# One stage for the last step of the third mixer branch and the output projection

## What is computed

```python
def rwkv7_group(p, ...):
    ...
    _, o = lax.scan(chunk_step, state0, xs)
    o = o.reshape(S, B, H, N).transpose(1, 0, 2, 3)
    mean = jnp.mean(o, axis=-1, keepdims=True)
    var = jnp.mean(jnp.square(o - mean), axis=-1, keepdims=True)
    o = ((o - mean) * lax.rsqrt(var + GN_EPS)).reshape(B, S, RWKV_WIDTH) * ln_g + ln_b
    bonus = jnp.sum(rh * kh * r_k, axis=-1, keepdims=True) * vh
    return (o + bonus.reshape(B, S, RWKV_WIDTH)) * g

def second_block(x, ...):
    ...
    y = jnp.concatenate([ya, yb.astype(x.dtype), yc.astype(x.dtype)], axis=-1)
    x = x + (y @ w_out[l]).astype(x.dtype)
    x = x + hier_moe(rms_norm_2(x, norm2_g[l]), ...)
```

## Time and profile before

| what | us |
|---|---|
| median of 3 runs | 2276.52 |
| lowest and highest of them | 2267.41, 2284.37 |
| the profiled execution | 2268.78 |
| its span, first to last instruction | 2266.9 |

### The profile page before, as it was taken

The page is one execution under the profiler, slowest core; times in us unless marked ns, Lnnn a source line. Parts: engine busy times, 40 slices in busy tenths (PEclk is TensorE's granted clock), DMA queues, the critical chain, the costliest instruction groups (busy, mean ns, idle before and its releaser), DMA issues. The chain is left out here.

```text
span 2266.9 us, 33009 instructions
## 1 busy us (share of the span) xinstructions
PE 2121.3 (94%) x12489; PEld 1633.1 (72%) x12489; DVE 1271.5 (56%) x1796; ACT 985.9 (43%) x1297; POOL 178.6 (8%) x178
## 2 busy tenths in 40 slices
PE   7988898999999999998999999998999789998998
PEld 5764334788888878888887888786577359777776
DVE  3357746443233244434666666888367755525888
ACT  2127636342123221121666665774253643414774
POOL 0010000000000000001211000012112210002111
PEclk9999989999999999999999999999999899998999
DMA  8008001243234135013887877995320000127996
GB/s 252 18 19 290 1 19 38 65 131 99 81 100 126 38 101 173 1 38 107 271 282 273 288 268 277 374 391 217 102 75 29 12 1 1 76 86 224 380 375 254
DMA packets 221008, 337.14 MB, mean 149 GB/s; under 512 B 50445, under 2 KB 135470, under 8 KB 220895
## 3 DMA queue, kind: packets, MB, share of 16 engines
q1 hardware_dynamic: 213758, 315.27, 41.0%
q0 software_dynamic: 7136, 20.34, 2.5%
HBM read 307.56 MB, written 26.95 MB: 148 GB/s over the span
## 5 line engine op out<-in xcount | busy, mean ns | idle before, releaser
L1550 DVE TENSOR_TENSOR moe_pass_wL<-moe_pass_w,moe_pass_wH 128x2048 fp32r<-128x2048 f32 (+1 forms) x144 | 303.3, 2112 | 113.6 <-ACT moe_pass_wH L1474 113.3
L1474 ACT ACTIVATE moe_pass_wH<-moe_pass_w 128x2048 fp32r<-128x2048 f32 (+1 forms) x144 | 254.7, 1772 | 129.8 <-PE PS L568 92.5
L1550 DVE TENSOR_TENSOR hm_pass_wL<-hm_pass_w,hm_pass_wH 128x2048 fp32r<-128x2048 f32 x60 | 135.8, 2286 | 37.0 <-ACT hm_pass_wH L1474 37.0
L566 PE MATMUL PS<-moe_pass_wL,moe_pass_xgH 128*128 128x512 f32 (+1 forms) x384 | 147.3, 384 | 7.4 <-DVE moe_pass_wL L1550 5.0
L568 PE MATMUL PS<-moe_pass_wH,moe_pass_xgH 128*128 128x512 f32 (+1 forms) x384 | 142.7, 372 | 0.0
L567 PE MATMUL PS<-moe_pass_wH,moe_pass_xgL 128*128 128x512 f32 (+1 forms) x384 | 142.6, 371 | 0.0
L568 PE MATMUL PS<-ffn_xH,ffn_upH 128*128 128x512 f32 x352 | 139.7, 397 | 0.0
L566 PE MATMUL PS<-xnT_low,ffn_upH 128*128 128x512 f32 x352 | 138.2, 393 | 0.3 <-PE PS L568 0.3
L567 PE MATMUL PS<-ffn_xH,ffn_up_low 128*128 128x512 f32 x352 | 137.3, 390 | 0.0
L73 PE MATMUL PS<-ones,ident 128*128 128x128 f32 x870 | 113.4, 292 | 12.4 <-PEq L42 12.4
L73 PEld LDWEIGHTS PS<-ones,ident 128*128 128x128 f32 x870 | 109.5, 206 | 17.1 <-issue 16.6
(11 more groups left out here) (851 smaller groups left out, 4885.9 us busy)
## 6 DMA issues: line engine op xcount, KB each, us to landing
moe_pass_w<-in_moe_w_down SPq DMA_DIRECT2D x40, 1024.0 KB
moe_pass_w<-in_moe_w_gate SPq DMA_DIRECT2D x32, 1024.0 KB
moe_pass_w<-in_moe_w_up SPq DMA_DIRECT2D x32, 1024.0 KB
hm_pass_w<-in_exp_w_gate SPq DMA_DIRECT2D x40, 512.0 KB, 7.5
hm_pass_w<-in_exp_w_up SPq DMA_DIRECT2D x40, 512.0 KB, 6.8
hm_pass_w<-in_exp_w_down SPq DMA_DIRECT2D x40, 512.0 KB
od_W<-in_od_w_in SPq DMA_DIRECT2D x12, 1024.0 KB, 8.4
moe_pass_w<-in_moe_w_gate SPq DMA_DIRECT2D x16, 768.0 KB
```

The costliest lines, as they stand in the source:

```text
L566: nc.tensor.matmul(out, lh, rl, start=start, stop=False)
L1474: nc.scalar.activation(wH[:, i % S, 0:n], w[:, i % R, 0:n], ACT.Copy).then_inc(s["high"], 1)
L1550: nc.vector.tensor_tensor(wL[:, i % S, 0:n], w[:, i % R, 0:n], f32(wH[:, i % S, 0:n]), ALU.subtract) \
```

## The change

`rwkv` loses its stage `rw_end`, and the call of `add_projection` for this mixer goes. A new function `end_and_project` does the work of both in one stage. The norm's arithmetic is the same, with the recurrence's tensors as scratch (`Bt`, `Kt`, `Rt`, `eL`). The order on each engine is new:

- SyncE loads the 8 weight tiles at the start, as before. GpSimd's one memset stays.
- ScalarE: squares, then the high parts of k = 0, 1, 2, then the norm's logarithms and exponentials, then the high parts of k = 3 to 7; those of k = 6 and 7 wait for the gated result.
- VectorE: centring, low parts 0, 1, 2, the Newton step (6 instructions), low parts 3 and 4, gain, offset and gate (6 instructions), low parts 5, 6, 7, then the additions to `x`.
- TensorE: the norm's sums in banks 6 and 7, with 6 dummy matmuls in bank 5 between them; then for k = 0 to 5 the products of banks 0 to 5; then k = 6 and 7 for banks 0 to 5, bank by bank; then all 8 k for bank 6 and for bank 7. The number of products is the same, 192. The dummy matmuls fall from 44 + 12 to 6, and one barrier goes.

```diff
--- before.py
+++ after.py
@@ -3178,11 +3178,9 @@
                                  rows=half, bank=h // 2 % 2, out=yT[:, 2 + h // 2]))
             attention(nc, C, "s_fox", jobs, lambda sp, s: prep.sync(sp, s, masks, D), prep)
         spare = [t.rearrange("p t (h c) -> p t h c", h=4) for t in (fq, fk, fk_even, fv)]
-        rwkv(nc, C, D, yT, xnT, pm, cols, prep, spare, At, Bt, Kt, Rt, al, gl, bonus, eLx, enL, eL, masks,
-             lambda sp: load_projection(sp, wouts, wout, come, range(KD)))
+        rwkv(nc, C, D, yT, xnT, pm, cols, prep, spare, At, Bt, Kt, Rt, al, gl, bonus, eLx, enL, eL, masks)
+        end_and_project(nc, C, yT, yL, wouts, woutsL, x, wout, come, At, Bt, Kt, Rt, eL, bonus, gl, cols)
         memF.close()
-        add_projection(nc, C, "s_out", yT, yL, wouts, woutsL, x, wout, come, KD)
         nc.clear_and_free_semaphores(list(loaded.values()) + come)
         nc.all_engine_barrier(sem_only=True)
...
-def rwkv(nc, C, D, yT, xnT, pm, cols, prep, spare, At, Bt, Kt, Rt, al, gl, bonus, eLx, enL, eL, masks, loads):
+def rwkv(nc, C, D, yT, xnT, pm, cols, prep, spare, At, Bt, Kt, Rt, al, gl, bonus, eLx, enL, eL, masks):
...
-        o = At
-        GN = 64e-5
...
+def end_and_project(nc, C, yT, yL, w, wL, x, source, come, o, centred, sq, rs, tt, bonus, gl, cols):
+    GN = 64e-5
+    LATE = (6, 7)
+    EARLY = range(6)
+    outs = [(t, h) for t in range(NT) for h in range(2)]
+    with ExitStack() as mem, stage(nc, "s_out", "meant centred squared summed logged rstd steps normed biased gated y_high w_high y_split w_split made") as (block, s):
+        def sb(n, shape, dt=F32):
+            return mem.enter_context(nc.sbuf_tensor("s_out_" + n, shape, dt))
+        yH, wH = sb("yH", [P, KD, SEQ], F32R), sb("wH", [P, KD, DM], F32R)
+        ec = sb("eps", [P, 2])
+        PS = C.PS
+        @block.sync
+        def _(sp):
+            load_projection(sp, w, source, come, range(KD))
+        @block.gpsimd
+        def _(pool):
+            nc.gpsimd.memset(ec[:, :], GN).then_inc(s["logged"], 1)
+        @block.tensor
+        def _(pe):
+            def product(n, k):
+                t, h = outs[n]
+                tok, cols_ = slice(t * P, (t + 1) * P), slice(h * 512, (h + 1) * 512)
+                return split_product(nc, PS[:, n, :], (yH[:, k, tok], yL[:, k, tok]), (wH[:, k, cols_], wL[k][:, cols_]), k == 0, k == KD - 1)
+            for i in range(2):
+                nc.tensor.matmul(PS[:, 6 + i, :], C.ones64[:, :], o[:, i], start=True, stop=True).then_inc(s["meant"], 1)
+            stay_busy(nc, C, 6, 5)
+            for i in range(2):
+                pe.wait_ge(s["squared"], i + 1)
+                nc.tensor.matmul(PS[:, 6 + i, :], C.ones64[:, :], sq[:, i], start=True, stop=True).then_inc(s["summed"], 1)
+            for k in EARLY:
+                pe.wait_ge(s["y_split"], k + 1)
+                pe.wait_ge(s["w_split"], k + 1)
+                for n in EARLY:
+                    product(n, k)
+            for k in LATE:
+                pe.wait_ge(s["y_split"], k + 1)
+                pe.wait_ge(s["w_split"], k + 1)
+            for n in EARLY:
+                for k in LATE:
+                    ins = product(n, k)
+                ins.then_inc(s["made"], 1)
+            for n in LATE:
+                for k in range(KD):
+                    ins = product(n, k)
+                ins.then_inc(s["made"], 1)
+        @block.scalar
+        def _(act):
+            def high(k):
+                if k in LATE:
+                    act.wait_ge(s["gated"], k - 5)
+                nc.scalar.activation(yH[:, k], yT[:, k], ACT.Copy).then_inc(s["y_high"], 1)
+                act.wait_ge(come[k], 16)
+                nc.scalar.activation(wH[:, k], w[k], ACT.Copy).then_inc(s["w_high"], 1)
+            act.wait_ge(s["logged"], 1)
+            nc.scalar.activation(ec[:, 1:2], ec[:, 0:1], ACT.Ln)
+            for i in range(2):
+                act.wait_ge(s["centred"], i + 1)
+                nc.scalar.activation(sq[:, i], centred[:, i], ACT.Square).then_inc(s["squared"], 1)
+            for k in (0, 1, 2):
+                high(k)
+            for i in range(2):
+                act.wait_ge(s["summed"], i + 1)
+                nc.scalar.activation(rs[:, i], PS[:, 6 + i, :], ACT.Ln, bias=ec[:, 0:1], scale=1.0 / HD).then_inc(s["logged"], 1)
+            for i in range(2):
+                act.wait_ge(s["logged"], i + 2)
+                nc.scalar.activation(rs[:, i], rs[:, i], ACT.Exp, scale=-0.5).then_inc(s["rstd"], 1)
+            for k in range(3, KD):
+                high(k)
+            nc.scalar.activation(C.root_of_one[:, :], C.one[:, :], ACT.Sqrt)
+        @block.vector
+        def _(dve):
+            def low(k):
+                dve.wait_ge(s["y_high"], k + 1)
+                nc.vector.tensor_tensor(yL[:, k], yT[:, k], f32(yH[:, k]), ALU.subtract).then_inc(s["y_split"], 1)
+                dve.wait_ge(s["w_high"], k + 1)
+                nc.vector.tensor_tensor(wL[k], w[k], f32(wH[:, k]), ALU.subtract).then_inc(s["w_split"], 1)
+            for i in range(2):
+                dve.wait_ge(s["meant"], i + 1)
+                nc.vector.scalar_tensor_tensor(out=centred[:, i], in0=PS[:, 6 + i, :], scalar=-1.0 / HD, in1=o[:, i], op0=ALU.mult,
+                                               op1=ALU.add).then_inc(s["centred"], 1)
+            for k in (0, 1, 2):
+                low(k)
+            for step in range(3):
                 for i in range(2):
+                    y, t = rs[:, i], tt[:, i]
+                    if step == 0:
+                        dve.wait_ge(s["rstd"], i + 1)
+                        ins = nc.vector.scalar_tensor_tensor(out=t, in0=PS[:, 6 + i, :], scalar=HD * GN, in1=y, op0=ALU.add, op1=ALU.mult)
+                    elif step == 1:
+                        dve.wait_ge(s["steps"], i + 1)
+                        ins = nc.vector.scalar_tensor_tensor(out=t, in0=t, scalar=-0.5 / HD, in1=y, op0=ALU.mult, op1=ALU.mult)
+                    else:
+                        dve.wait_ge(s["steps"], i + 3)
+                        ins = nc.vector.scalar_tensor_tensor(out=y, in0=t, scalar=1.5, in1=y, op0=ALU.add, op1=ALU.mult)
+                    ins.then_inc(s["steps"], 1)
+            for k in (3, 4):
+                low(k)
+            for i in range(2):
+                dve.wait_ge(s["steps"], i + 5)
+                nc.vector.scalar_tensor_tensor(out=centred[:, i], in0=centred[:, i], scalar=cols["rlg"][:, i:i + 1], in1=rs[:, i], op0=ALU.mult,
+                                               op1=ALU.mult).then_inc(s["normed"], 1)
+            for i in range(2):
+                dve.wait_ge(s["normed"], i + 1)
+                nc.vector.scalar_tensor_tensor(out=centred[:, i], in0=centred[:, i], scalar=cols["rlb"][:, i:i + 1], in1=bonus[:, i],
+                                               op0=ALU.add, op1=ALU.add).then_inc(s["biased"], 1)
+            for i in range(2):
+                dve.wait_ge(s["biased"], i + 1)
+                nc.vector.tensor_tensor(yT[:, 6 + i], centred[:, i], gl[:, i], ALU.mult).then_inc(s["gated"], 1)
+            for k in (5, 6, 7):
+                low(k)
+            for n, (t, h) in enumerate(outs):
+                dve.wait_ge(s["made"], n + 1)
+                dst = x[:, t, h * 512:(h + 1) * 512]
+                nc.vector.tensor_tensor(dst, PS[:, n, :], dst, ALU.add)
```

More of the change, by code:

```diff
@@ L3623, in _ @@
                                                     ALU.add).then_inc(s["rows"], 1)
-        o = At
-        GN = 64e-5
[L3628 to L3644, removed]
-                for i in range(2):
[L3646 to L3695, removed]
```

## The result

The changed kernel takes 2264.6 us (median of 13 runs, 2258.2 to 2269.9), against 2276.5 before. The ratio is 0.9947, with a 95% interval of 0.9934 to 0.9960. So it is faster by about half a percent, 12 us, which is less than the 1% named above, and was forecast as such.

The account below looks back on a forecast made before the run. TensorE's 192 matmuls were taken to bound the projection, its start set by norm, barrier and first split on other engines. Starting 11.9 us earlier, with length and tail unchanged, turns 2276.5 into 2264.6 us; range 2251 to 2277.

Parts of the forecast that it names:

- The first product: TensorE's first projection matmul, forecast at 1958.05 in place of 1969.99, about 6.7 us after the first weight load's issue.
- up to 0.35 earlier: Upper bound at TensorE's start: first weights landing 0.35 us earlier would move it to 1957.7, a gain of 12.3.
- No wait of TensorE: Once started, TensorE runs all 192 projection matmuls without a wait, in 44.6 us; smallest slack 2.5.
- The slack at k = 3: Low part of k = 3, ready at 1968.1 and wanted by TensorE at 1970.65: slack 2.5 us.
- No table load between a logarithm and a high part: On ScalarE, none expected; a load of 1.28 per function change would cut the gain to 10.6 us.
- The late order: Up to 24 matmuls in a row adding into one bank: 0.2337 us each assumed, with 1.6 us possible extra.
- The tail: From the last product's start to the end of VectorE's additions: stays 1.13 us.
- The sum: First product at 1958.05 in place of 1969.99: 11.9 us less, 2276.5 to 2264.6, a share of 0.52%.
- Rival (a): Weight tiles land together and late, TensorE waits 4.6 us at k = 1: gain 7.3; chance 0.08.
- Rival (b): TensorE's clock falls to half at the products' start, costing 3.2 us: gain 8.8, 2267.8; chance 0.10.
- Rival (c): Norm in VectorE's list delays k = 3, TensorE waits 4.3 us: gain 7.6, 2268.9; chance 0.07.
- Rival (d): Slower than before, if 62 or more of TensorE's 192 matmuls run at half clock; chance 0.02.

Follow-up runs that it names:

- the first profile: The first profiled execution of the unmodified changed kernel; span 2263.0 us, first product 6.26 us after the stage's start.
- the experiment in which ScalarE waited 0.93 for it: Changed kernel plus two unused VectorE instructions behind the Newton step; first product at 7.30 us, last at 51.53.
- The eight more instructions: Changed kernel plus eight unused 128x512 VectorE instructions behind the Newton step; first product at 6.88 us, last at 54.80.
- the order with the norm first: Changed kernel with ScalarE and VectorE doing the whole norm before any split; ratio to before 1.0007; with 44 dummies added, last product at 63.37 us.

## Why the prediction was right

**The first product.** Forecast 6.72 after the stage's start, measured 6.26 in the first profile and 6.78 in the second. The split's own chain was right. The term that moves is the landing of the first weight tile: 3.7 in the first profile, where ScalarE had no wait for it, 4.2 in the forecast, and 4.8 in the experiment in which ScalarE waited 0.93 for it. The bound "up to 0.35 earlier" was too narrow by 0.1, and the start varied by 1.0 between executions of kernels that differ in nothing ahead of it.

**No wait of TensorE.** Right: 44.64 from first to last. The slack at k = 3 was forecast as 2.5. In the first profile the low part ends at 1973.42 and is wanted at 1962.77 + 54 x 0.2337 = 1975.39, so it is 1.97; the chain ran as forecast, and TensorE had begun earlier. The eight more instructions showed that what exceeds the slack is paid: 5.8 more cost 3.6, with a slack of 2.2 to 2.5 in executions that began as late.

**No table load between a logarithm and a high part.** Right, as ScalarE's rows show; the only load in the middle is the exponential's, 1.28.

**The late order** costs nothing: 5.60 for 24 matmuls into one bank. The allowance of 1.6 for it was not needed.

**The tail** stayed 1.13: from 2007.41 to 2007.85 + 0.69. The barrier behind it took 1.32 (1.34 before).

**The sum.** 11.94 forecast for the stretch, 12.42 measured in the profile, 12.0 +- 0.6 over all runs at equal clock. That the two medians differ by just 11.9 is partly luck, as executions of one kernel spread over 12 to 22 us.

**Rival (a)**, weights late and together: not seen, though the tiles land less evenly than assumed. The second came 2.0 us behind the first, not 1.28, and `wH[1]` waited 0.34 for it. The slack at k = 1 covered that: the low part was done at 1964.55 and wanted at 1966.97. **Rival (b)**, half clock at the start: not seen in any of the six profiles with the interleaved order, even without dummies. It was seen twice in the order with the norm first, where it cost 1.7 (first nine steps 3.87) and 1.5 (first eight 3.48). So the mechanism is real. Its size, forecast as 3.2 from a stretch with 16 products at half clock, was twice too large: here there were seven or eight. Why the interleaved order was spared is not shown; its pauses ahead of the first product were 2.25 at most, against 12.13 and 2.31, but one of 3.44 between products did no harm either. The Trainium skill's page "TensorE: Matmul & The Clock Gate", in "What's actually happening", has activity release the half rate. The trace agrees in the norm-first order (half clock after 12.13 us of idling); in the interleaved order no run here shows a cost of the 50 dummies dropped. Activity alone was no protection, though: half clock also came 2.31 us after 10 us of dummies. **Rival (c)**, the norm holding up TensorE, needs more than 2 us of further delay, and then it costs just the excess. **Rival (d)** had no trace at all. Its time for all 192 at half rate is added up wrongly in the prediction: a loss of 37 on 2264.6 gives 2301.6, and not 2289.7, which takes the 11.9 off twice. The point from which (d) decides, 62 matmuls, is not touched by it, and no chance rests on it. Its "within 7 us" for the clock's return isn't in the earlier trace rows either, which end at half clock; in the norm-first runs full steps were back after nine and eight products.

## What to carry to other kernels

Where an engine's dense stretch waits for a chain of small steps on other engines, look for that part of its input which doesn't need the chain, and write the chain between the pieces of it on those engines; merging the stages without doing that was worth 0.2 us, as the 1.5 of its earlier start went into steps at half clock. Count the slack at each hand-over beforehand: here the chain could grow by 1.4 us at no cost, and 5.8 cost 3.6, the excess over the smallest slack. Read a local change by its own stretch and not by the difference of two spans, which here showed 3.9 of 12.4.

## What was not expected of the hardware

- The granted clock differs from execution to execution by enough to hide half a percent. In nine profiles the stage began between 1951.3 and 1963.6 us with the same work ahead of it, and 0.001 of mean clock went with 1.7 us.
- Ten microseconds of dummy matmuls didn't protect the clock when they ended 2.3 us ahead of the real ones, and a wait of 3.44 us between products in another execution did no harm.
- The same 192 matmuls at the same granted clock of 1.00 took 44.64 us from first to last start in some executions and 44.23 in others, with no wait in either.
- A load of 256 KB landed 3.9 us after its issue, inside the range of one of 512 KB at the same place (3.6 to 4.8).
